# The output and down projections accumulate in two PSUM banks each, which the vector engine adds

## The reference

```python
n = rmsnorm(h, g_mix)
q, k, v, qi, ki, wi, qb, kb, vb, gb, rb, uc, vc = split_proj(n @ w_in)
... # three parallel head groups: sparse attention, gated linear attention, spatial gating
h = h + jnp.concatenate([o_a, o_b, o_c], axis=-1) @ w_out
n2 = rmsnorm(h, g_ffn)
h = h + (jax.nn.silu(n2 @ w_ffn_gate) * (n2 @ w_ffn_up)) @ w_ffn_down
gate = jax.nn.sigmoid(rmsnorm(h, g_ple) @ w_ple_gate)
h = h + gate * (p_l @ w_ple_proj)
```

## Time and profile before

| | |
|---|---|
| time, median of 3 runs | 1514.41 us (1506.89 to 1518.28) |
| profiled execution, its span from first to last instruction | 1504.9 us |
| PE busy | 1448.3 us, 96% of the span |
| DVE busy | 817.4 us, 54% |
| ACT busy | 536.8 us, 36% |
| DMA | 238.94 MB, 159 GB/s |

### The profile page before, as it was taken

One profiled execution on the slowest core, in us unless ns is written; L12 is line 12 of the kernel. 1 busy time (PEld: TensorE's weight loads), 2 busy tenths in 40 slices (PEclk: granted clock), 3 DMA queues, 4 the chain that ended last, 5 costly groups with the idle time before them and its releaser, 6 DMA issues.

```text
span 1504.9 us, 26899 instructions
## 1 busy us (share of the span) xinstructions
PE 1448.3 (96%) x10722; PEld 1405.5 (93%) x10722; DVE 817.4 (54%) x928; ACT 536.8 (36%) x474; POOL 125.5 (8%) x164
## 2 busy tenths in 40 slices
PE   4997999999989999999999999999999999999998
PEld 4995888888989999999999999999999999999998
DVE  7443664455367755555555444455555556666554
ACT  4333562236442243333333333333333332223432
POOL 4001202221112200000000000000000001111000
PEclk9998999899999999999999999999999999999999
DMA  6456534233254444444444445544444444445443
GB/s 222 166 146 171 168 131 166 73 130 129 89 207 161 165 154 162 163 166 165 166 167 160 159 168 170 188 163 162 162 161 164 166 145 153 155 158 184 157 180 129
DMA packets 40904, 238.94 MB, mean 159 GB/s; under 512 B 5760, under 2 KB 7936, under 8 KB 19872
## 3 DMA queue, kind: packets, MB, share of 16 engines
q1 hardware_dynamic: 34784, 224.59, 42.9%
q0 software_dynamic: 3184, 10.37, 2.2%
q10 hardware_dynamic: 2896, 3.40, 1.2%
HBM read 232.49 MB, written 5.86 MB: 158 GB/s over the span
## 4 chain that ended last, share of the span: by engine, by line
PE 84%; DVE 7%; issue 3%; DMA 3%; ACT 2%; POOLq 0%; DVEq 0%; POOL 0%; SPq 0%; ACTq 0%
PE acc L386 26%; PE acc L388 26%; PE acc L387 25%; DVE w_lo L361 3%; DMA ki_s<-in_cache_ik 1%; DVE x_lo L848 1%; DVE tmp L1145 1%; DVE n_hi L1146 1%; DMA out_gla_s<-proj 1%; ACT w_hi L354 1%; PE px L1459 1%; PE px L1396 1%; PE px L1344 1%; DVE h L1141 0%; PE px L1345 0%
## 5 line engine op out<-in xcount | busy, mean ns | idle before, releaser
L361 DVE TENSOR_TENSOR w_lo<-w_raw,w_hi 128x2048 fp32r<-128x2048 f32 (+2 forms) x225 | 479.4, 2131 | 249.6 <-ACT w_hi L354 231.8
L354 ACT ACTIVATE w_hi<-w_raw 128x2048 fp32r<-128x2048 f32 (+2 forms) x225 | 399.5, 1776 | 490.6 <-PE acc L388 467.7
L386 PE MATMUL acc<-n_hi,w_hi 128*128 128x288 f32 x1664 | 493.0, 296 | 3.1 <-DVE w_lo L361 2.7
L388 PE MATMUL acc<-n_hi,w_lo 128*128 128x288 f32 x1664 | 494.0, 297 | 0.0
L387 PE MATMUL acc<-n_lo,w_hi 128*128 128x288 f32 x1664 | 485.9, 292 | 0.0
L387 PEld LDWEIGHTS acc<-n_lo,w_hi 128*128 128x128 f32 x1664 | 317.9, 191 | 0.1
L386 PEld LDWEIGHTS acc<-n_hi,w_hi 128*128 128x128 f32 x1664 | 313.2, 188 | 4.1 <-DVE w_lo L361 3.4
L386 PE MATMUL acc<-x_hi,w_hi 128*128 128x288 f32 x928 | 283.0, 305 | 33.3 <-DVE w_lo L853 19.3
L388 PEld LDWEIGHTS acc<-n_hi,w_lo 128*128 128x128 f32 x1664 | 312.5, 188 | 0.0
L388 PE MATMUL acc<-x_hi,w_lo 128*128 128x288 f32 x928 | 278.5, 300 | 0.0
L387 PE MATMUL acc<-x_lo,w_hi 128*128 128x288 f32 x928 | 274.8, 296 | 0.0
(11 more groups left out here) (243 smaller groups left out, 824.1 us busy)
## 6 DMA issues: line engine op xcount, KB each, us to landing
w_raw<-in_w_gu SPq DMA_DIRECT2D x88, 1024.0 KB, 4.8
w_raw<-in_w_down SPq DMA_DIRECT2D x64, 704.0 KB, 4.0
w_raw<-in_w_in SPq DMA_DIRECT2D x41, 1024.0 KB, 4.9
w_raw<-in_w_ple SPq DMA_DIRECT2D x16, 1152.0 KB, 5.1
w_raw<-in_w_out SPq DMA_DIRECT2D x16, 1024.0 KB, 4.8
proj<-in_xT SPq DMA_DIRECT2D x4, 576.0 KB, 6.5
proj<-in_cache_k POOLq DMA_DIRECT2D x16, 128.0 KB, 3.9
proj<-in_cache_v POOLq DMA_DIRECT2D x16, 128.0 KB, 3.0
```

The source lines that it names most:

```text
L354: nc.scalar.activation(whi[:, j, 0:kt * P], raw[:, j, 0:kt * P], ACT.Copy).then_inc(S("w_hi_done"), 1)
L361: nc.vector.tensor_tensor(wlo[:, j, 0:kt * P], raw[:, j, 0:kt * P], whi[:, j, 0:kt * P].bitcast(F32), ALU.subtract).then_inc(S("w_lo_done" ...
L386: nc.tensor.matmul(out, w_h, m_hi_[:, k0 + k, :], start=first and k == 0, stop=False)
L388: ins = nc.tensor.matmul(out, w_l, m_hi_[:, k0 + k, :], start=False, stop=last and k == kt - 1)
```

## The change

In `out`, `down0` and `down1` a tile's matmuls no longer go into one bank. They go in turn into `acc[:, j]` and `px[:, 2 + j]`, a bank that these phases did not use, each matmul into the other bank than the one before it. `products_in_turn` does it; the first matmul into each bank starts its sum, the last into each ends it. The number of matmuls, their operands and their order stay. In `tile_into_h` DVE adds `acc` to `h`, waits for that by a `link`, then adds `px` to `h`; this second add now raises `acc_read`. `in`, `up0`, `up1` and `ple` keep their single bank.

```diff
--- before.py
+++ after.py
@@ -380,12 +380,26 @@
 
         def products(out, j, k0, kt, m_hi_, m_lo_, first=True, last=True, at=0):
 
+            if isinstance(out, tuple):
+                return products_in_turn(out, j, k0, kt, m_hi_, m_lo_, first, last, at)
             for k in range(kt):
                 w_h = whi[:, j, (at + k) * P:(at + k + 1) * P]
                 w_l = wlo[:, j, (at + k) * P:(at + k + 1) * P]
                 nc.tensor.matmul(out, w_h, m_hi_[:, k0 + k, :], start=first and k == 0, stop=False)
                 nc.tensor.matmul(out, w_h, m_lo_[:, k0 + k, :], start=False, stop=False)
                 ins = nc.tensor.matmul(out, w_l, m_hi_[:, k0 + k, :], start=False, stop=last and k == kt - 1)
+            return ins
+
+        def products_in_turn(banks, j, k0, kt, m_hi_, m_lo_, first, last, at):
+
+            n, total = 3 * k0 if not at else 3 * at, 3 * kt
+            for k in range(kt):
+                w_h = whi[:, j, (at + k) * P:(at + k + 1) * P]
+                w_l = wlo[:, j, (at + k) * P:(at + k + 1) * P]
+                for q, (w_, m_) in enumerate(((w_h, m_hi_), (w_h, m_lo_), (w_l, m_hi_))):
+                    at_ = 3 * k + q
+                    ins = nc.tensor.matmul(banks[(n + at_) % 2], w_, m_[:, k0 + k, :], start=first and at_ < 2,
+                                           stop=last and at_ >= total - 2)
             return ins
 
         def out_s(r):
@@ -1138,7 +1152,8 @@
             def tile_into_h(m, bank, last_group, tile, gain, lk):
                 dve.wait_ge(S("w_used"), last_group)
                 hm = one(h, m)
-                V.tensor_tensor(hm, hm, acc[:, bank, 0:T], ALU.add).then_inc(S("acc_read"), 1)
+                lk(V.tensor_tensor(hm, hm, acc[:, bank, 0:T], ALU.add))
+                V.tensor_tensor(hm, hm, px[:, 2 + bank, 0:T], ALU.add).then_inc(S("acc_read"), 1)
                 if gain is None:
                     return
                 dve.wait_ge(S("acc_read"), tile)
@@ -1170,7 +1185,7 @@
                 dve.wait_ge(S("state_stored"), 16 * 3)
                 tile_into_h(i * 2 + j, j, i * 2 + (b0 + j + 1), i * 2 + (t0 + j + 1), 1, lk)
 
-            rounds("out", into_h, 4)
+            rounds("out", into_h, 6)
             for hf in range(HALVES):
                 ub, ut = stream[f"up{hf}"][0], tile0[f"up{hf}"]
 
@@ -1194,7 +1209,7 @@
                 db, dt = stream[f"down{hf}"][0], tile0[f"down{hf}"]
                 gain = 2 if hf == HALVES - 1 else None
                 name = f"down{hf}"
-                per = 0 if gain is None else 4
+                per = 2 if gain is None else 6
                 with dve.Fori(0, N_OUT // 2 - 1) as i, link.each(i, N_OUT // 2 - 1, per) as lk:
                     split_lo(dve, name, i * 2, 1)
                     split_lo(dve, name, i * 2 + 1, 0)
@@ -1547,16 +1562,19 @@
 
             tile_free("out", 0, 2, 0)
             pe.wait_ge(S("w_lo_done"), N_IN + 1)
+            def pair_of(j):
+                return acc[:, j, 0:T], px[:, 2 + j, 0:T]
+
             for c in range(4):
                 pe.wait_ge(S("m_ready"), c + 1)
-                ins = products(acc[:, 0, 0:T], 0, 4 * c, 4, m_hi, m_lo, first=c == 0, last=c == 3, at=4 * c)
+                ins = products(pair_of(0), 0, 4 * c, 4, m_hi, m_lo, first=c == 0, last=c == 3, at=4 * c)
             ins.then_inc(S("w_used"), 1)
             tile_free("out", 0, 2, 1)
-            group("out", 0, 1, acc[:, 1, 0:T], 0, KT, m_hi, m_lo)
+            group("out", 0, 1, pair_of(1), 0, KT, m_hi, m_lo)
             with pe.Fori(1, N_OUT // 2) as i:
                 for j in range(2):
                     tile_free("out", i, 2, j)
-                    group("out", i, j, acc[:, j, 0:T], 0, KT, m_hi, m_lo)
+                    group("out", i, j, pair_of(j), 0, KT, m_hi, m_lo)
             def behind_norm(name, n, hi_, lo_):
 
                 tile_free(name, 0, 2, 0)
@@ -1585,7 +1603,7 @@
                     for kk in range(2):
                         if isinstance(i, int) and kk == 1:
                             pe.wait_ge(S("a_ready"), FH * (hf + 1))
-                        group(f"down{hf}", i * 2 + j, kk, acc[:, j, 0:T], kk * DK, DK, a_hi, a_lo,
+                        group(f"down{hf}", i * 2 + j, kk, pair_of(j), kk * DK, DK, a_hi, a_lo,
                               first=kk == 0, last=kk == 1)
 
                 pe.wait_ge(S("a_ready"), FH * hf + DK)
```

## The result

| | before | changed |
|---|---|---|
| median of 20 runs | 1514.43 us (1506.21 to 1519.67) | 1520.49 us (1513.6 to 1525.88) |
| ratio to before | | 1.0047, 95% interval 1.0033 to 1.0061 |
| span of the profiled execution | 1504.9 us | 1524.2 us |

The change costs 0.47%, +7.1 us (+5.0 to +9.2), where +9.0 was forecast. It is less than the 1% that the prediction took as what a measurement can tell, but 20 runs each make it clear. The ratio is estimated over all the runs; the quotient of the two medians is 1.0040, 6.1 us, and lies inside its interval.

A forecast was written before the change was run, and what follows sets the result against it. The prediction took PE's matmul count times their start distance as the bound, with DVE counting only where PE waits. Terms 8.4 + 0.6 + 0 = +9.0 us raised the median from 1514.4 to 1523.4 us, range 1500 to 1531.

The forecast's parts named there:

- The matmuls: 0: In `out`, `down0` and `down1`, changing the bank at each of 2880 matmuls leaves their 132 ns distance unchanged: 0 us.
- `down1`: 14 x 0.60 = 8.4 us: In the loop of `down1`, the second add delays a low part PE waits for, 14 times by 0.60 us: +8.4 us.
- `out`, first tile: +0.6 us: At the first tile of `out`, emptied late after a DMA, the second add delays PE by one step: +0.60 us.
- The loop of `out`: 0, the narrowest cover: In the loop of `out`, the low part still ends before PE needs it, with 0.10 us left: 0 us.
- `down0` and the last tiles: 0: Second adds on 16 tiles of `down0` end before the next low part; `down1`'s last tiles are covered in `ple`: 0 us.
- the bank as a brake: Rival: alternating banks makes each matmul start 12 ns sooner, together -13.5 us, 1501 us; chance 0.11.
- a price for changing it: Rival: each matmul that switches PSUM bank starts 8 ns later, together +27.8 us, 1542 us; chance 0.10.
- The second add costs nothing: Rival: DVE's second add adds no visible waiting, or something else sets the 14 waits: 1514 us; chance 0.05.

The follow-up runs named there:

- the matmuls alone: Changed kernel with matmuls still alternating between two banks, but DVE adding only the first bank to h: 1513.57 us, ratio 0.9995.
- the reordered one: Kernel before, with the low part of a tile's odd group made ahead of the emptying in both down passes (reached every second one): 1509.5 us, ratio 0.9972.
- The third add: Changed kernel with one more add of px to h per tile: 1531.77 us, ratio 1.0131 to the kernel before.
- the new order: Low part of every odd group of both down passes made ahead of the emptying: 1504.65 us in the kernel before, 1507.26 us in the changed kernel.

## Why the prediction was right, point by point

**The matmuls: 0.** Right, to 0.02 us in 1056 matmuls. It rested on four places at which the kernel already changed banks in the middle of a stream, with steps of 0.13 and 0.14 us. The kernel with the matmuls alone shows it apart from everything else. The rule of the Trainium skill ("TensorE: Matmul & The Clock Gate", "Back-to-back issue gap") that gives 122.5 ns for 288 columns doesn't describe this stream, with two banks or with one; with 256 columns it would give 109.2 ns by the same formula, an estimate by that page, and the trace reads 119.9 ns. The prediction passed over that the page gives this formula for an isolated matmul and says itself that a stream with a weight load for each matmul is paced by both; so the 9 ns were never a saving that the page promised.

**`down1`: 14 x 0.60 = 8.4 us.** Right in place and count, 14 waits before and after; the size of the step was off. It is 0.48 us, and the term 6.7 us. I had taken the step from L1141 to L1145, in the looped form, and left the unrolled pair's 0.49 us as the lower bound. The stream of DVE tells the two apart, and it was there to be read: ahead of L1145 in the loop stands an `ISA` instruction that carries the wait, with a register instruction ahead of it; the second add carries its wait itself (`[waits dve_step]` in its own row), like the unrolled ones. All adds of that form, in eight traces, follow at 0.48 to 0.49 us; L1160 starts 0.60 us behind its add in the loops, with the instructions ahead of it, and 0.49 us in the unrolled tiles, without them. That the placing of the wait is the cause is read from this agreement and not from a kernel of its own.

**`out`, first tile: +0.6 us.** The wait of PE grew by 0.66 us in the profiled execution, some of it chance, since it starts with a DMA. What the prediction didn't see is that a longer wait there can lower the granted clock afterwards. The wait before the third group and the time of that group, from first to last start, in the 13 traces that have the wait: in the seven kernels with the single add at this place PE's starts are 2.37 to 2.96 us apart there, and the group took 6.31 or 6.32 us five times and 7.6 to 7.7 us twice; in the six with the second or third add they are 3.14 to 3.72 us apart, and it took 6.31 us once and 7.87 to 9.04 us five times. The means are 6.7 and 8.3 us. That would be about 1.6 us more from the change, on average. But the length of the wait doesn't decide it alone: with starts 2.69 us apart the clock stayed at 1.00 in the kernel with the change in `down1` and fell to 0.80 in the reordered one, and with 3.14 us it stayed. And it goes with what came before: six of the nine traces with the low stretch ahead of `out` have the fall, and one of the four without. The times of the runs can't confirm the 1.6 us: the change in `out` alone gave 1.0017, with 0.5 us and 2.1 us both inside its interval, and 6.7 + 0.5 is 7.2 us, already the 7.1 us of the whole change, while 8.8 us is still inside too.

The mean granted clock of each run tells more. Span x (1 - clock) is an estimate of the time that the run lost to the low level. In 215 runs of the kernels of this study the time follows this loss one for one within a kernel (slope 1.00), and taking it off cuts the scatter from 3.3 to 1.2 us. What is left grew by 7.5 us (7.0 to 8.1) with the change, for 6.7 + 0.5 in the two terms, and by 0.5 us (-0.2 to 1.2) with the change in `out` alone; differences under 1 us are at the edge of what this can tell, since the kernel with the matmuls alone reads +0.7 and that with `down0` alone +0.9, where no trace shows anything. The loss itself was 25.3 us in the 68 runs with more than one add in `out` and 24.4 us in the 141 others with the old order there: 0.9 us more (0.0 to 1.8). So 1.6 us is possible, a smaller share is likelier, and whether any of it belongs to the change stays open.

**The loop of `out`: 0, the narrowest cover.** Right; since the step was 0.48 and not 0.60 us, the slack that stayed was 0.25 us up to the low part's end and not 0.15. The third add shows the edge: with 0.49 us more it was used up.

**`down0` and the last tiles: 0.** Right, `down0` by the kernel that has the change there alone. At the end of `down1` the last group's start is 0.46 us later, and the first group of `ple` has that much less to wait, as said.

**The rivals.** Neither the bank as a brake nor a price for changing it is left. "The second add costs nothing" is right for two of three phases and, in the new order, for all.

## What to carry to other kernels

Before spreading a sum over more banks, look for a place in the trace where the bank already changes within a stream: if the step there is that of its neighbours, the matmuls don't wait for their bank, and what is left of the change is the extra read. Price an added instruction by what is queued behind it on its engine: here 48 equal adds cost 0.48 us each at the 14 places ahead of an operand that TensorE waited for, about as much once in `out`, and nothing behind slack. And where such a wait shows, move the operand's preparation ahead of the emptying before anything else; that order alone gained 7 us here and made the extra add free in `down1`. And before reading a difference between two profiled executions, compare their granted clock stretch by stretch: here it made most of the 9.2 us in a phase that the change didn't touch.

## What the runs showed of the hardware

- On VectorE an instruction that waits for the 128 x 288 add before it starts 0.03 us behind its end where the wait stands in the instruction itself, and some 0.15 us behind where a queue instruction ahead of it carries the wait: 0.48 and 0.60 us from start to start in the same tile.
- fp32r matmuls with a new weight load each keep 132 ns for 288 columns at the full clock, whether the PSUM bank stays or changes at each one, and 120 ns for 256 (with one bank): some 12 to 13 ns over the columns' time at 2.4 GHz.
- A wait of TensorE costs more than itself: the first matmul behind it is followed after 0.23 to 0.24 us and not 0.13, even where it started only 0.05 us late. Ending 14 such waits, 7.1 us, gave back 8.6 us.
- An idle time of PE of 2.97 us was followed by a granted clock of 0.66 over the next group, and such a fall cost up to 2.7 us, four times the 0.66 us by which the wait itself had grown. In the same place in other kernels, 2.39 us was followed by 1.00 in one trace and by 0.80 in another, and 2.84 us by 1.00.
- Most of the spread between runs of one kernel is the granted clock: means of 0.980 to 0.990, and 1 us of run time for each 1 us lost to it.
